# Differential attention on one NeuronCore: a head's sums of squares go to VectorE, and a softmax division goes into the norm's epsilon

## The reference

```python
s = jnp.where(allowed, s + bias[None, :, None], -jnp.inf)
p = jax.nn.softmax(s, axis=-1)
attn = p[:, :, 0] - lam_full * p[:, :, 1]
o = jnp.einsum('bhqk,bkhe->bqhe', attn, vb)
o = o * lax.rsqrt(jnp.mean(o * o, axis=-1, keepdims=True) + SUBLN_EPS)
o = o * subln_g.astype(jnp.float32) * (1.0 - lambda_init)
outs.append(o.reshape(bsz, Q_BLOCK, c).astype(x.dtype))
...
return jnp.concatenate(outs, axis=1) @ w_o
```

## Time and profile before

| what | value |
|---|---|
| median of three runs | 1301.03 us |
| span of the profiled execution, first to last instruction | 1299.6 us |
| PE busy | 1269.2 us (98%) |
| DVE busy | 894.2 us (69%) |
| ACT busy | 679.4 us (52%) |
| POOL busy | 83.8 us (6%) |
| PE in the chain of waits that ended last | 83% |
| DVE, ACT in that chain | 9%, 6% |

### The profile page before, as it was taken

The page is one execution under the profiler, slowest core; times in us unless marked ns, Lnnn a source line. Parts: engine busy times, 40 slices in busy tenths (PEclk is TensorE's granted clock), DMA queues, the critical chain, the costliest instruction groups (busy, mean ns, idle before and its releaser), DMA issues.

```text
span 1299.6 us, 23670 instructions
## 1 busy us (share of the span) xinstructions
PE 1269.2 (98%) x10054; PEld 1098.1 (84%) x10059; DVE 894.2 (69%) x1467; ACT 679.4 (52%) x1228; POOL 83.8 (6%) x103
## 2 busy tenths in 40 slices
PE   9999999999999999999999999999999999999997
PEld 6978888889967888888898997888897987788886
DVE  6886666674685666656898848666668366766666
ACT  6874444463584454544663434444455477445452
POOL 3000500000060000000001600000000000000000
PEclk9999999999999999999999999999999999999999
DMA  9445454544412555553443003654555441455550
GB/s 351 159 184 200 184 190 184 188 188 166 165 62 81 200 195 194 194 195 130 164 161 131 5 36 114 219 193 188 195 194 194 176 161 61 187 194 194 195 194 33
DMA packets 17496, 214.45 MB, mean 165 GB/s; under 512 B 1960, under 2 KB 2128, under 8 KB 4720
## 3 DMA queue, kind: packets, MB, share of 16 engines
q1 hardware_dynamic: 15888, 205.43, 41.9%
q0 software_dynamic: 1504, 7.52, 1.6%
HBM read 211.87 MB, written 1.06 MB: 164 GB/s over the span
## 4 chain that ended last, share of the span: by engine, by line
PE 83%; DVE 9%; ACT 6%; issue 1%; DMA 1%; SPq 0%; DVEq 0%; ACTq 0%
PE psum L696 25%; PE psum L670 14%; PE psum L676 7%; PE psum L486 4%; PE psum L487 4%; PE psum L488 4%; DVE w_low L1996 3%; ACT w_high L1443 2%; PE psum L1054 2%; PE psum L1198 1%; PE psum L585 1%; PE psum L1245 1%; PE psum L1373 1%; PE psum L581 1%; PE psum L577 1%; PE psum L1069 1%
## 5 line engine op out<-in xcount | busy, mean ns | idle before, releaser
L1996 DVE TENSOR_TENSOR w_low<-ring,w_high 128x1024 fp32r<-128x1024 f32 x372 | 443.4, 1227 | 188.5 <-ACT w_high L1443 188.5
L1443 ACT ACTIVATE w_high<-ring 128x1024 fp32r<-128x1024 f32 x372 | 372.7, 1048 | 139.7 <-PE psum L696 105.4
L696 PE MATMUL psum<-w_high,up_split 128*128 128x512 f32 x1024 | 287.6, 391 | 0.8 <-DVE up_split L2151 0.8
L696 PEld LDWEIGHTS psum<-w_high,up_split 128*128 128x128 f32 x1024 | 190.3, 188 | 40.5 <-issue 2.7
L670 PE MATMUL psum<-act_split,w_high 128*128 128x512 f32 x768 | 191.6, 391 | 0.0
L696 PE MATMUL psum<-w_low,up_split 128*128 128x512 f32 x512 | 163.2, 390 | 0.0
L670 PEld LDWEIGHTS psum<-act_split,w_high 128*128 128x128 f32 x768 | 139.6, 189 | 26.0
L1544 ACT ACTIVATE up_split<-work 128x256 fp32r<-128x256 f32 x112 | 46.8, 418 | 159.4 <-DVE work L2144 148.8
L486 PE MATMUL psum<-act_split,w_high 128*128 128x256 f32 x448 | 129.1, 288 | 0.3 <-DVE act_split L2162 0.3
L487 PE MATMUL psum<-act_split,w_high 128*128 128x256 f32 x448 | 126.7, 283 | 0.0
L488 PE MATMUL psum<-act_split,w_low 128*128 128x256 f32 x448 | 126.7, 283 | 0.0
(11 more groups left out here) (360 smaller groups left out, 1873.7 us busy)
## 6 DMA issues: line engine op xcount, KB each, us to landing
ring<-weights SPq DMA_DIRECT2D x95, 2048.0 KB, 7.5
work<-rows POOLq DMA_DIRECT2D x4, 1024.0 KB, 5.1
ring<-weights SPq DMA_DIRECT2D x4, 512.0 KB, 8.4
work<-rows POOLq DMA_DIRECT2D x4, 512.0 KB, 5.4
x<-x_in SPq DMA_DIRECT2D x2, 512.0 KB, 4.7
work<-t_bias POOLq DMA_DIRECT2D x1, 1024.0 KB, 8.4
out<-x SPq DMA_DIRECT2D x4, 256.0 KB, 2.1
con<-consts SPq DMA_DIRECT2D x1, 576.0 KB, 22.0
```

Of the source, the lines that this page charges most:

```text
L696: last = mm(bank(acc[(th, n)]), up_split[:, m, a, P * th:P * th + P], w[:, f], start=start and i == 0, stop=stop and i == len(pairs) - 1, ...
L1443: A(high[:, HIGH_SLOT[name], f], ring[:, n % RING, f], ACT.Copy).then_inc(weights_high, 1)
L1996: V.tensor_tensor(low[:, n % RING, f], ring[:, n % RING, f], high[:, HIGH_SLOT[name], f].bitcast(f32), ALU.subtract).then_inc(weights_spli ...
```

## The change

The sums of squares leave ACT. DVE gets a new step `head_squares(u)`: it copies the head's output from PSUM to `da_heads`, frees the bank, squares both halves with row sums, and adds the epsilon term. ACT's `head_normed(u)` waits for that (`da_squares`), takes logarithm and exponential, and scales `da_heads` in place. `head_mix(u)` no longer multiplies the first softmax by its reciprocal sum; it computes 128 * eps * S1 * S1 and (minus lambda) * S1 / S2 on two-column tiles instead. PE's `out_transposes(u)` waits for the scaled head (`da_scaled`) where it waited for the bank.

```diff
@@ PE, out_transposes(u)
-                read_out(pe, TURN[("dpv", u)])
+                pe.wait_ge(sig("da_scaled"), u + 1)
@@ ACT
             def head_normed(u):
-                q = TURN[("dpv", u)]
-                filled(q)
-                for th in range(2):
-                    ins = A(buf(DA_SQ)[:, th * P:th * P + P], bank(q)[:, th * P:th * P + P], ACT.Square,
-                            accum_out=small[:, SM_HSQ + 2 * u + th:SM_HSQ + 2 * u + th + 1])
-                done(ins, "da_sq")
-                settle()
+                act.wait_ge(sig("da_squares"), u + 1)
                 sq, r = small[:, SM_HSQ + 2 * u:SM_HSQ + 2 * u + 2], small[:, SM_HR + 2 * u:SM_HR + 2 * u + 2]
-                done(A(r, sq, ACT.Ln, scale=1.0 / P, bias=small[:, SM_HEPS:SM_HEPS + 1]), "da_log")
+                done(A(r, sq, ACT.Ln, scale=1.0 / P), "da_log")
                 settle()
                 done(A(r, r, ACT.Exp, scale=-0.5), "da_rstd")
                 settle()
                 for th in range(2):
-                    ins = A(da_heads[:, u, th, :], bank(q)[:, th * P:th * P + P], ACT.Copy,
-                            scale=small[:, SM_HR + 2 * u + th:SM_HR + 2 * u + th + 1])
-                taken(ins, q)
+                    s = da_heads[:, u, th, :]
+                    ins = A(s, s, ACT.Copy, scale=small[:, SM_HR + 2 * u + th:SM_HR + 2 * u + th + 1])
+                done(ins, "da_scaled")
@@ DVE
             def head_mix(u):
                 dve.wait_ge(sig("da_probs"), 2 * u + 2)
                 at = SM_SUM + (u % 4) * 4
-                step(V.reciprocal(small[:, at:at + 4], small[:, at:at + 4]))
+                first, second = small[:, at:at + 2], small[:, at + 2:at + 4]
+                step(V.reciprocal(second, second))
                 settle()
-                step(V.tensor_scalar(small[:, at + 2:at + 4], small[:, at + 2:at + 4], nlam, None, ALU.mult))
-                for th in range(2):
-                    s = da_s[:, u % 4, 0, P * th:P + T * th]
-                    ins = V.tensor_scalar(s, s, small[:, at + th:at + th + 1], None, ALU.mult)
-                step(ins)
+                step(V.scalar_tensor_tensor(small[:, SM_HE + 2 * u:SM_HE + 2 * u + 2], first, P * SUBLN_EPS, first,
+                                            ALU.mult, ALU.mult))
+                step(V.scalar_tensor_tensor(second, first, nlam, second, ALU.mult, ALU.mult))
                 settle()
...
+            def head_squares(u):
+
+                q = TURN[("dpv", u)]
+                filled(q)
+                taken(V.tensor_copy(da_heads[:, u, :, :].rearrange("p a d -> p (a d)"), bank(q, T)), q)
+                settle()
+                for th in range(2):
+                    o = da_heads[:, u, th, :]
+                    ins = V.scalar_tensor_tensor(buf(DA_SQ)[:, th * P:th * P + P], o, 1.0, o, ALU.mult, ALU.mult,
+                                                 accum_out=small[:, SM_HSQ + 2 * u + th:SM_HSQ + 2 * u + th + 1])
+                step(ins)
+                settle()
+                sq = small[:, SM_HSQ + 2 * u:SM_HSQ + 2 * u + 2]
+                done(V.tensor_tensor(sq, sq, small[:, SM_HE + 2 * u:SM_HE + 2 * u + 2], ALU.add), "da_squares")
@@ DVE's list
             for u in range(1, 4):
                 head_mix(u - 1)
                 head_logits(u)
+                head_squares(u - 1)
                 if u > 1:
                     split("da_o0", [2 * u - 4, 2 * u - 3])
...
+            head_squares(3)
             head_mix(4)
...
             head_mix(7)
+            head_squares(7)
             out_low(6)
             out_low(7)
```

More of the change, by code:

```diff
@@ L280, in build @@
         SM_MAX, SM_SUM, SM_FAC, SM_CMAX, SM_CSUM = 448, 472, 496, 520, 576
-        SM_HSQ, SM_HR, SM_HEPS = 568, 584, 600
+        SM_HSQ, SM_HR, SM_HE = 568, 584, 600
         SM_NLAM, SM_GSUB, SM_LAM, SM_BGATE, SM_SP = 560, 562, 564, 566, 568
@@ L2648, in _ @@
             step(V.memset(da_bias[0:64, :, 0:64], -MASKED))
-            step(V.memset(small[:, SM_HEPS:SM_HEPS + 1], SUBLN_EPS))
             step(V.tensor_scalar(small[:, SM_GSUB:SM_GSUB + 1], col("subln_g"), 1.0 - LAMBDA_INIT, None, ALU.mult))
@@ L2708, in _ @@
             out_low(3)
+            head_squares(4)
             head_mix(5)
@@ L2712, in _ @@
             out_low(4)
+            head_squares(5)
             head_mix(6)
@@ L2716, in _ @@
             out_low(5)
+            head_squares(6)
             head_mix(7)
+            head_squares(7)
             out_low(6)
```

## The result

The changed kernel takes 1305.03 us (median of 22 runs) against 1301.86 us for the kernel before (22 runs): a ratio of 1.0026, with a 95% interval of 1.0019 to 1.0034. By the ratio that is 3.4 us more (2.5 to 4.4), where the forecast was 2.03 us more, 1303.1 us, within 0.2%. The difference is small but real, and the time lies just beyond the upper end of the range, 1305.0.

What follows compares the result with a forecast made beforehand. The prediction took PE, busy 98% of the span, as the bound. Head 3's +1.50 us and head 7's +0.53, with no clock difference, took 1301.03 to 1303.1 us; 8-in-10 range 1301.3 to 1305.0.

Steps and rivals of the forecast that it cites:

- What bounds it: Whole kernel: PE is busy 98% of the span, so only what makes PE wait or run slowly moves the end.
- Head 3: DVE's squares delay quarters and mix: transposes 2.9 us late, 1.4 regained from ACT, values 1.50 us later.
- The squares: DVE's head_squares step (copy, two squares, addition, settles): 1.28 us per head, with ends at 1.1 and 1.7.
- Rival 2: Squares on DVE at their upper price, 1.7 us each: +3.2 us, 1304.2 us; chance 0.12.
- Head 7: out_low(6) stands behind the squares of the last head, so PE's chunk 6 is late by 0.53 us (0.35 to 0.95).
- Heads 4 to 6 cost nothing: DVE's 1.15 us idle per head and the 0.33 shorter mix cover the 1.28 of squares: no cost.
- Rival 3: ACT's relief decides at head 3, if its mix ends before 1069.9: faster, 1298.5 to 1300.3 us; chance 0.06.
- Rival 4: All hidden: the clock does not fall although PE waits longer, giving back 1.5 us, 1301.6 us; chance 0.09.
- The clock: After PE's gap at head 3: same fall to 1.2 GHz at the same price (up to 1.7 us), zero difference.
- The argument from the norm: A similar PE gap at the norm, 2.3 of 4.5 us idle, is not followed by a clock fall.
- Sum: Whole kernel: +1.50 at head 3 and +0.53 at head 7 make +2.03 us, 1303.1 us.
- Rival 1: Longer gap costs a second 1.2 GHz stretch, or a fall the median run lacked: +3.5 us, 1304.5 us; chance 0.21.

Runs made afterwards that it cites:

- Wait only: Kernel before, plus only a DVE wait for the values of heads 1 and 2 ahead of the weight quarters; 1303.48 us against 1302.07, ratio 1.0013.
- quarters first: Changed kernel with the two weight quarters ahead of the squares in DVE's loop; 1300.70 us against 1302.07 for the kernel before, ratio 0.9992.
- both orders: Changed kernel with the edits of quarters first and last head's order together; 1299.68 and, on another chip, 1300.25 us, ratios 0.9978 and 0.9989 to the kernel before.
- filled: Unused zero matmuls in PE's gap at head 3; ratios to the plain kernel before: changed kernel 1.0008 and 0.9999, kernel before 0.9984.
- division kept: As both orders, but the first softmax's division stays in the head mix; 1302.37 us against 1303.74 for the kernel before, ratio 0.9986.
- last head's order: Changed kernel with out_low(6) ahead of the squares of head 7; 1303.51 us against 1302.07 for the kernel before, ratio 1.0017.

## Why the prediction was wrong, point by point

- **What bounds it: right.** PE's waits and its clock carry the whole difference. DVE's added work costs nothing where PE doesn't wait for it.
- **Head 3: right.** Forecast +1.50 for the values, measured +1.46; the transposes 2.9 late, measured 2.79. The idle ACT gave 1.33 of it back (1.91 to 0.58), forecast 1.4. *Wait only* and *quarters first* show the cause from both sides. A mix takes 1.26 (1071.21 to 1072.47), forecast 1.35.
- **The squares: a little too dear.** Forecast 1.28, measured 1.17 (1067.85 to 1069.02). The copy took 0.42 as chosen, but a square took 289 ns where I put the 352 of a mix. The readouts overlap. Rival 2 is out.
- **Head 7: right.** PE's listed wait is 0.35, but matmuls overlap (0.39 long, 0.23 from start to start), so the delay is read from starts: chunk 6 starts 1.61 us after the last values pair of head 7 (line 1342) before and 2.13 in the changed kernel, 0.52 later, forecast 0.53. To line 556 the tail has lost 0.57.
- **Heads 4 to 6 cost nothing: right** in the changed kernel. From the values of head 3 to those of head 7 it even takes 0.28 less (22.15 against 22.43), with the stretch at 1.2 GHz in another place; why it is less no run isolates. That is what the heads' sum lacks of the forecast: 1.46 + 0.57 - 0.28 = 1.75. But the cover was thin: head 4's mix is late by 0.5 as soon as head 3 is early (*quarters first*, *both orders*), and by 0.7 in both kernels as soon as the fall is gone (*filled*).
- **Rival 3 is out here**, since its condition failed: head 3's mix ends 7.25 us after the zero point, 1071.3 on the clock of the kernel before, where it had to end by 1069.9. In *both orders* it ends at 4.99, or 1069.0, and there the price is met: PE waits 0.72 for the copy, no fall follows, and the kernel takes 1299.68 and 1300.25 us, inside the 1298.5 to 1300.3 that I gave this rival. Part of that is the shorter mix (*division kept*) and not ACT's relief.
- **Rival 4 is out.** The fall at head 3 is in both profiles of the changed kernel and in that of *last head's order*.
- **The clock: this step failed.** I wrote "the same fall with the same price, and zero difference". The two profiles bear that out at head 3, but a profile is one draw. Over the runs the changed kernel has 0.8 more stretches at 1.2 GHz than the kernel before, worth about 1.1 us. I left this at zero though my first rival named it, and a fall in only some executions should have entered the sum as a share, not as yes or no. The argument from the norm was weak too: the gap there is followed by no fall in the earlier trace rows, but by one in eight of the thirteen profiles.
- Sum: heads 1.75 (forecast 2.03) + clock 1.1 (forecast 0) = 2.9; forecast 2.03, measured 3.4. The remaining 0.5 is inside the interval. That the time left the range took a second step, the base: the kernel before has a median of 1301.86 over 22 runs, where three runs had shown 1301.03. From the old base, 3.4 more would have been 1304.4, inside the range. Rival 1 comes nearest to the difference (3.5), but by luck in part: it added a whole stretch to every execution.

The share of the clock rests on mean clocks over many runs and on filled kernels whose gain differed between two chips. The counts by kernel tie most falls beyond the common ones to the idle time at head 3. They don't pin the changed kernel's 0.8 to it: as filled, on the one chip where both ran, it still has 0.8 more than the filled kernel before (3.1 against 2.2), on another chip 2.0. Open are why the same instructions meet one fall at head 3 or two, why falls between 733 and 783 us and at the norm come in some executions, and whether the new gap makes those at the norm likelier. Open is also an idle time of 1.9 to 2.2 us on PE at about 780 us (ahead of line 1245), for which the profile shows no releaser. Eight of the thirteen profiles have it, of kernels of either kind, and in five of them a fall follows.

## What to carry to other kernels

In a queue that runs in order, put new work that waits behind the old work that doesn't need that wait: moving two steps here turned +0.26% into -0.1 to -0.2%. Ask of every added wait what is queued behind it, and whose cover that was. Where PE's gap grows, count a fall of the clock with a chance and a price taken from several executions; one profile says only what happened once.

## What the runs showed of the hardware that I had not expected

- The granted clock of one kernel varies from run to run, and the time with it: for the kernel before on one chip (35 runs) from 0.993 to 0.997, and from 1299.1 to 1306.9 us.
- Zero matmuls in a gap, over before the operand came, kept the clock up at no cost to the chain in three profiles of three: the filled kernel before ran at 0.9984 (0.9971 to 0.9998) of the unfilled.
- SCALAR_TENSOR_TENSOR on 128x128 fp32 takes 289 ns with one tensor as both inputs and the constant 1.0, and 352 with two tensors and a column; which of the two differences counts, no run tells. The groups by shape of the changed kernel, 1040 to 1110 us:

```profile
L2687 DVE SCALAR_TENSOR_TENSOR work<-work 128x128 f32<-128x128 f32 x16 | 4.0, 289 | 0.3
```

- On ACT, the logarithm of two columns takes 203 ns without a bias column (line 1903) and 296 with one (line 1909 of the kernel before), eight times each.
